# Blocks 1 to 3 of a streaming encoder layer: the mixer's input projection computed as pairs of seven half-size products

## The chip, the core and the metric

The kernel runs on one core of a Trainium2 chip. A core has TensorE (PE, matrix products into PSUM), VectorE (DVE), ScalarE (ACT), GpSimd (POOL), and SyncE (SP), which here issues the loads. Each engine works through its own queue in order; they meet only at semaphores. The metric is device time of one execution in microseconds, the median of several runs.

## What is computed

One layer over 2048 prompt frames and 32 sample frames, model width 1024, all in float32:

```
n = rmsnorm(x) * g_mix
pool_in 512 | q 512 | k 128 | v 128 | gate_p 1024 | gate_a 1024 = n @ w_in      (3328 columns)
pool = trailing means over 2/4/8/16 frames minus the frame, @ w_pool, * pool_scale
attn = chunked attention with sinks (8 heads, 2 KV heads, chunks of 64), own and previous chunk
h = x + (sigmoid(gate_p) * pool + sigmoid(gate_a) * (attn @ w_attn_up)) @ w_out
h = h + relu(rmsnorm(h) @ w_up)^2 @ w_down                                       (hidden 4096)
y = rmsnorm(h) * g_fin
```

The reference also returns the newest keys, values and pooling inputs.

## The kernel before, in words

Features lie on partitions, frames along the free axis. The prompt is cut into four blocks of 512 frames; block 0 also carries the 32 sample frames (544 columns). Each block runs a mixer (everything up to h) and then an MLP.

Every float32 operand of a product is split in a high and a low part: ScalarE copies it rounded (`split_high`, `copy`), VectorE subtracts (`split_low`, `low`), and TensorE makes three products, high x high, high x low, low x high (`three`, line 512 for the matmuls).

**The mixer** (`mixer_product`, `step`, list `MIXER`) goes through 42 units: 26 tiles of the input projection, 8 of attention up together with the pooling product, 8 of the output. A unit's weights are 128x1024 (or 128x640), loaded by SP into one of four raw places, split into one of two slots of `wm`, and multiplied by `nH`, `nL` (x times g_mix, split). A tile of the input projection takes 8 x 3 matmuls of 512 columns; its result is scaled by the inverse root `rms` when VectorE takes it out of PSUM (`scale_gate`, `xp_out`); q and k are copied and rotated with tables scaled by `rms`. Attention steps lie between the units (`between`).

**The MLP of block 0** is made of plain products of the same kind. Meanwhile GpSimd forms sums of quarters of the MLP's weights (`sum_weights`), two units to a sum of four quarters, ScalarE and VectorE split part of them, and ScalarE's queue writes them to `weight_sums` and `weight_split` in memory.

**The MLP of blocks 1 to 3** uses a Strassen-like scheme: a pair of weight tiles and both halves of frames and of input features give seven products of half size instead of eight. One such product is a token: 4 x 3 matmuls of 256 columns (lines 731 to 733). A phase has 28 tokens (`ORDER`), there are eight phases (four up, four down). Weights come through a ring of eight places `wring`; a token's raw quarter is 128x512, split by ScalarE eight tokens ahead and by VectorE seven ahead, unless it was written split. Operands are combined from quarters and split (`n7H`, `n7L`, `m7H`, `m7L`). Seven products of a pair pass through three pieces of PSUM, and products 6, 3, 7, 4 wait for what ScalarE copied or VectorE added of the products before.

During the last down phase the next block's x is prepared: squares, inverse root (`invert_part`), x times g_mix split into `nH`, `nL` (`gained_low`, line 1229), angles scaled. GpSimd multiplies y of a finished block by its inverse root (line 1686) at the start of the next mixer and does the pooling.

Of the kernel before, what the change touches and what calls it, by code (L numbers as in the profile page):

```python
# [6 lines left out]
F32 = mybir.dt.float32  # L7
F32R = mybir.dt.float32r
ALU = mybir.AluOpType
# [35 lines left out]
def mixer_plan(out_order):  # L45
    plan = [("qkv", m) for m in range(6)] + [("xp", m) for m in range(G)] + [("gp", m) for m in range(KD)]
    for m in range(KD):
        plan += [("ga", m), ("ao", m)]
    return plan + [("out", m) for m in out_order]


MIXER = mixer_plan(range(KD))
PLAN = [MIXER] + [mixer_plan(ORD)] * (NB - 1)
# [5 lines left out]
ROPE_LOAD = 16  # L59
# [4 lines left out]
Y_STORES = (2, 3, 4, 5)  # L64
POOLED = KD - G
ATT0 = 7

# [15 lines left out]
HALF = (0, 0, 1, 0)  # L83
SHIFT = (0, 4, 0, 4)
# [3 lines left out]
def presplit(ph, pr):  # L88
    return ph in SPLIT_PHASES and pr in (5, 6, 7)


def build(nc, x0, x123, weights, consts, vectors, tables, state_s, kcache_t, vcache, kold, vold,
          y0, y123, k_new, v_new, p_new, k_old_out, v_old_out, ks_new, vs_new, ps_new):
    with ExitStack() as ctx:
# [26 lines left out]
        def own(name, shape, dt=F32):  # L121
# [22 lines left out]
        rope = place("rope", [P, 2, CMAX], n_tail)  # L144
        qbuf = place("qbuf", [P, NJ * CMAX], n_tail + 8 * CMAX)
        pr = place("pr", [P, 2, 4 * P], n_tail + 24 * CMAX)
        prT = place("prT", [P, 2, 4 * P], n_tail + 24 * CMAX + 4096)
        n7H, n7L = (place(f"n7{x}", [P, 7, PAIRS, HT], at_n + i * n7_bytes, F32R) for i, x in enumerate("HL"))

        midH, midL = place("midH", [P, KD, CMAX], at_m, F32R), place("midL", [P, KD, CMAX], at_m + n_bytes, F32R)  # L150
        m_tail = at_m + 2 * n_bytes
# [5 lines left out]

        half_bytes = RING * QW * 4
        wring = place("wring", [P, RING, 2, QW], at_w, F32R)
        wm = [place(f"wm{h}", [P, 2, 2, WIDTH], at_w + h * half_bytes, F32R) for h in range(2)]  # L160
        xbs = [place(f"xb{h}", [P, 3, XWMAX], at_w + h * half_bytes) for h in range(2)]
        diffs = [place(f"diff{h}", [P, XWMAX], at_w + h * half_bytes + 12 * XWMAX) for h in range(2)]
# [15 lines left out]
        qC = qbuf[:, 0:NJ * TB].rearrange("p (c j n) -> p c j n", c=NC, j=NJ)  # L178
        qS = qbuf[:, NJ * TB:].rearrange("p (j n) -> p j n", j=NJ)
# [50 lines left out]
        set_out = [sem(f"set_out{i}") for i in range(2)]  # L230
        prod_done = sem("prod_done")
# [22 lines left out]
        plain = [("x", 0), ("h", 0)] + [("x", b) for b in later]  # L254
        s_nH = Signal("gained_high", [(*n, k) for n in plain for k in range(KD)])
        s_nL = Signal("gained_low", [(*n, k) for n in plain for k in range(KD)])
        s_tab = Signal("angles_scaled", [(b,) for b in blocks])
        s_fg = Signal("final_gained", [(b, tile_at("f", b, k)) for b in blocks[:-1] for k in range(KD)])
        s_y = Signal("y_normed", [(b, k) for b in blocks for k in range(KD)])
        s_tmp = Signal("qk_copied", [(b, i) for b in blocks for i in range(NJ + 1)])  # L260
        s_vn = Signal("v_normed", [(b,) for b in blocks])
# [5 lines left out]
        s_xb = Signal("pool_in_copied", groups)  # L267
# [15 lines left out]
        s_gz = Signal("gate_scaled", [(b, kind, m) for b in blocks for kind in ("gp", "ga") for m in range(KD)])  # L283
# [15 lines left out]
        s_SL = Signal("weight_sums_low", split_pairs)  # L299


        out_pairs = [(b, j) for b in later for j in range(PAIRS)]
        s_g = Signal("h_gained", [(b, m) for b in later for m in ORD])
        s_gT1, s_gT3, s_gT2, s_gT4 = (Signal(f"h_{n}", out_pairs) for n in ("T1", "T3", "T2", "T4"))
        s_gH2, s_gL2, s_gH5, s_gL5 = (Signal(f"h_{n}", out_pairs) for n in ("first_high", "first_low", "rest_high", "rest_low"))
# [16 lines left out]
        splits = []  # L322
        for b in blocks:
            splits += [("mix", b, i) for i in range(M_MLP)]
            if b == 0:
                splits += [("plain", 0, n) for n in range(2 * KD * NQ)]
            else:
                splits += [("tok", b, t) for t in range(TOKENS) if not presplit(t // NT7, ORDER[t % NT7][1])]
# [13 lines left out]
        for b in later:  # L342
            for t in range(TOKENS):
                if presplit(t // NT7, ORDER[t % NT7][1]):
                    landed[(t + SHIFT[b]) % RING] += 16
                    ring_count[b, t] = landed[(t + SHIFT[b]) % RING]
        set_count, landed = {}, [0, 0]
        for p in range(PHASES * PAIRS):
            landed[p % 2] += 32 if p // PAIRS in SPLIT_PHASES else 16
            set_count[p] = landed[p % 2]  # L350

        def is_split(b, t):
            return presplit(t // NT7, ORDER[t % NT7][1])

        def raw_tokens(b, lo, hi):
            return [t for t in range(lo, hi) if t < TOKENS and not is_split(b, t)]

        def ring_slot(b, t):
            return (t + SHIFT[b]) % RING
# [9 lines left out]

        def unit_row(b, i):  # L370
            return MIXER.index(PLAN[b][i])

        def mlp_row(q, down, tile):
            return M_MLP + 2 * KD * q + KD * down + tile

# [1452 lines left out]
```

## Time and profile before

| | us |
|---|---|
| median of 3 runs | 2358.72 (2357.66 to 2358.92) |
| profiled execution | 2357.24 |
| its span | 2355.5 |

| engine | busy in the span |
|---|---|
| PE | 2325.8 (99%) |
| DVE | 1642.3 (70%) |
| ACT | 1091.6 (46%) |
| POOL | 388.0 (16%) |

The span runs from the first to the last instruction. Matmuls are pipelined: the time of one row of a matmul is longer than the distance between two starts, and the distance is what counts. An engine's mean share says nothing of single stretches.

### The profile page before, as it was taken

What the parts mean: (1) busy time and instruction counts of PE and PEld (TensorE: products, weight loads), DVE (VectorE), ACT (ScalarE), POOL (GpSimd) and SP (SyncE); (2) the same over time, 40 slices, a digit from 0 to 9 for tenths busy, and PEclk for the clock granted to TensorE, in tenths of its full rate; (3) what the DMA queues carried; (4) which work ended last, traced back from release to release, by engine and by line L of the source; (5) the groups of instructions that cost most, each with busy time, mean ns of one, the idle gap of its engine ahead of it and who ended that gap; (6) DMA issues with size and microseconds to landing.
All of it is one profiled execution on the core that took longest, in us unless ns stands there. A gap on an engine that the chain in (4) does not pass through costs nothing.

```text
span 2355.5 us, 41198 instructions
## 1 busy us (share of the span) xinstructions
PE 2325.8 (99%) x16389; PEld 2159.7 (92%) x16389; DVE 1642.3 (70%) x2438; ACT 1091.6 (46%) x1922; POOL 388.0 (16%) x296
## 2 busy tenths in 40 slices
PE   8999999999999999999999999999999999999997
PEld 8999999999987889999987788999998778999996
DVE  7645766465885568778687557876788656867866
ACT  4533434233535346456554435654463534645542
POOL 0500364563634000000013200000003400000000
PEclk9999999999999999999999999999999999999998
DMA  4223465565652237767653235767674223676774
GB/s 161 78 74 101 170 225 187 202 240 179 220 192 66 87 116 246 237 202 230 226 201 117 76 103 171 229 226 246 200 264 145 77 88 114 206 228 200 237 231 169
DMA packets 149167, 410.38 MB, mean 174 GB/s; under 512 B 17521, under 2 KB 17873, under 8 KB 144881
## 3 DMA queue, kind: packets, MB, share of 16 engines
q1 hardware_dynamic: 136752, 349.71, 45.2%
q10 hardware_dynamic: 12224, 58.04, 6.6%
q8 instruction: 131, 2.15, 0.4%
q14 instruction: 60, 0.48, 0.1%
HBM read 349.65 MB, written 58.13 MB: 173 GB/s over the span
## 4 chain that ended last, share of the span: by engine, by line
PE 94%; DVE 3%; DMA 2%; ACT 0%; issue 0%; POOL 0%; SPq 0%; DVEq 0%; ACTq 0%; POOLq 0%
PE prod L512 50%; PE auxB L731 8%; PE auxB L733 8%; PE auxB L732 8%; PE prod L731 6%; PE prod L732 6%; PE prod L733 6%; DMA wring<-weight_split 1%; PE auxB L512 1%; PE auxA L614 1%; PE auxB L644 1%; PE auxB L628 1%; DVE acc L1211 0%; PE auxA L512 0%; DVE wm L1188 0%
## 5 line engine op out<-in xcount | busy, mean ns | idle before, releaser
L512 PE MATMUL prod<-nH,wm 128*128 128x272 f32 (+1 forms) x3104 | 718.7, 333 | 7.9 <-DVE nL L1229 7.9
L512 PEld LDWEIGHTS prod<-nH,wm 128*128 128x128 f32 x3104 | 497.9, 188 | 67.9 <-DVE wm L1188 8.1
L775 ACT ACTIVATE wm<-raw 128x1024 fp32r<-128x1024 f32 x232 | 235.7, 1016 | 667.2 <-PE prod L512 660.9
L512 PE MATMUL prod<-nL,wm 128*128 128x272 f32 (+1 forms) x1552 | 438.4, 331 | 0.0
L775 ACT ACTIVATE wring<-rawq 128x512 fp32r<-128x512 f32 x492 | 303.2, 628 | 273.1 <-PE auxB L733 170.1
L1188 DVE TENSOR_TENSOR wring<-rawq,wring 128x512 fp32r<-128x512 f32 x492 | 334.6, 684 | 99.9 <-PE auxB L733 78.3
L1188 DVE TENSOR_TENSOR wm<-raw,wm 128x1024 fp32r<-128x1024 f32 x232 | 305.2, 1316 | 59.5 <-ACT wm L775 58.7
L512 PE MATMUL prod<-midH,wm 128*128 128x272 f32 (+1 forms) x1664 | 335.0, 313 | 2.1 <-DVE midL L1188 1.6
L512 PEld LDWEIGHTS prod<-nL,wm 128*128 128x128 f32 x1552 | 263.4, 189 | 26.6 <-issue 0.5
L512 PEld LDWEIGHTS prod<-midH,wm 128*128 128x128 f32 x1664 | 253.2, 188 | 20.2 <-DVE midL L1188 1.8
L731 PE MATMUL auxB<-m7H,wring 128*128 128x256 f32 x768 | 218.2, 284 | 3.0 <-DMA wring<-weight_split 2.9
L731 PE MATMUL auxB<-n7H,wring 128*128 128x256 f32 x768 | 218.2, 284 | 0.0
L733 PE MATMUL auxB<-n7H,wring 128*128 128x256 f32 x768 | 217.4, 283 | 0.0
L732 PE MATMUL auxB<-n7L,wring 128*128 128x256 f32 x768 | 217.4, 283 | 0.0
L732 PE MATMUL auxB<-m7L,wring 128*128 128x256 f32 x768 | 217.4, 283 | 0.0
L733 PE MATMUL auxB<-m7H,wring 128*128 128x256 f32 x768 | 217.3, 283 | 0.0
L512 PE MATMUL prod<-midL,wm 128*128 128x272 f32 (+1 forms) x832 | 208.3, 313 | 0.0
L1686 POOL TENSOR_TENSOR hT<-hT,acc 128x512 f32<-128x512 f32 (+1 forms) x24 | 42.1, 1788 | 949.4 <-DVE acc L1216 949.4
L731 PE MATMUL prod<-m7H,wring 128*128 128x256 f32 x576 | 164.3, 285 | 0.1
L731 PE MATMUL prod<-n7H,wring 128*128 128x256 f32 x576 | 164.2, 285 | 0.0
L733 PE MATMUL prod<-n7H,wring 128*128 128x256 f32 x576 | 163.0, 283 | 0.0
L732 PE MATMUL prod<-n7L,wring 128*128 128x256 f32 x576 | 163.0, 283 | 0.0
(174 smaller groups left out, 4521.1 us busy)
## 6 DMA issues: line engine op xcount, KB each, us to landing
raw<-weights SPq DMA_DIRECT2D x200, 512.0 KB, 3.5
wring<-weight_split SPq DMA_DIRECT2D x180, 512.0 KB, 4.4
rawq<-weights SPq DMA_DIRECT2D x288, 256.0 KB, 4.3
rawq<-weight_sums SPq DMA_DIRECT2D x204, 256.0 KB, 4.2
weight_split<-wsplit ACTq DMA_DIRECT2D x20, 1536.0 KB, 5.9
weight_sums<-wsum ACTq DMA_DIRECT2D x12, 1024.0 KB, 5.7
raw<-weights SPq DMA_DIRECT2D x32, 320.0 KB, 2.8
y<-hT ACTq DMA_DIRECT2D x12, 512.0 KB, 2.8
```

Of the source, the lines that this page charges most:

```text
L512: ins = nc.tensor.matmul(out[:, s, 0:hi - lo], lhs, rhs[:, lo:hi], start=first, stop=last)
L614: ins = nc.tensor.matmul(bank[:, at:at + P], q, keys[:, :, t * CH:(t + 1) * CH], start=True, stop=True)
L628: ins = nc.tensor.transpose(auxB[:, 1, i * P:(i + 1) * P], pr[:, c % 2, i * P:(i + 1) * P], ident)
L644: ins = nc.tensor.matmul(auxB[feats, 0, 0:2 * P], v[:, c // 2, feats], prT[:, c % 2, 2 * g * P:2 * (g + 1) * P], start=True, stop=True)
L731: nc.tensor.matmul(out, wh, xh, start=kp == 0 and r in (1, 2, 5), stop=False, skip_group_check=True)
L732: nc.tensor.matmul(out, wh, xl, start=False, stop=False, skip_group_check=True)
L733: ins = nc.tensor.matmul(out, wl, xh, start=False, stop=kp == PAIRS - 1, skip_group_check=True)
L775: return nc.scalar.activation(out, in_, ACT.Copy, scale=scale)
L1188: return tt(out, x, f(high), ALU.subtract)
L1686: tt(hT[:, k, 0:n], hT[:, k, 0:n], acc[:, 0:n], ALU.mult).then_inc(s_y.sem, 1)
```

## The change

In blocks 1 to 3 the 26 tiles of the input projection become 13 pairs (`WIN`) of seven products of 256 columns. The MLP's ring now runs through the mixer too: 123 tokens, 91 of these products, 8 for pooling, 8 for attention up, 16 halves of output tiles, in an order given by keys (`mixer_tokens`). Places such as `ROTATE_AT` and `ATT_AT` say after which token the rotations and attention steps come.

GpSimd forms four sums for each of 13 pairs during block 0's mixer (`sum_mix_weights`), and ScalarE's queue writes them out unsplit; they are split in the ring like any quarter. For that block 0 orders its gates in pairs, x's place and others serve as working places, and x is loaded a second time (`x_again`) before the output products, in each block.

x is first multiplied by its inverse root on GpSimd (`norm_x`, 8 tiles; at the end of block 0 four of them stand behind each of the weight sums 28 and 29 of 0 to 31), then by the gain, and combined and split in seven operand parts in the last down phase. Products are therefore no longer scaled when they are taken out; results are put together from copies by ScalarE and additions by VectorE in place. The MLP's presplit sums go out in two transfers, high and low.

```diff
+WIN = [("qkv", 0), ("qkv", 2), ("qkv", 4), ("xp", 0), ("xp", 2)] + [("gp", m) for m in (0, 2, 4, 6)] + [
+    ("ga", m) for m in (0, 2, 4, 6)]
+OFFSET = {1: 0, 2: 1, 5: 2, 6: 3, 3: 5, 7: 6, 4: 11}
+def mixer_tokens():
+    for p in range(NPAIR):
+        for r, off in OFFSET.items():
+            keyed.append((1.4 + 0.1 * r if p == 1 and r in (1, 2) else 7 * p + off, ("win", p, r)))
...
+ATT_AT = [place_of(31 + 4 * n) for n in range(NC + 2)]
+ROTATE_AT = [place_of(key) for key in (7, 13, 15, 20, 23)]
+GAIN_AT = (13, 16, 19, 22)
...
+            def win_token(b, i, p, r):          # TensorE
+                weights_here(b, i)
+                if r == 1:
+                    if p >= 2:
+                        wait(pe, s_m3, b, p - 2)
...
+                if r == 2 and p >= 2:
+                    wait(pe, s_m01, b, p - 2)
+                if r in (5, 6, 3, 7, 4) and r != 5:
+                    wait(pe, {6: s_m1, 3: s_m5, 7: s_m0, 4: s_m2}[r], b, p)
...
+            def win_step(b, p, r):              # ScalarE
+                if r == 1:
...
+                    elif p == 2:
+                        wait(act, s_q, b, 1)
...
+                    copy(first[:, HT:TB], mix_a(p)).then_inc(s_m1.sem, 1)
...
+            def win_step(b, p, r):              # VectorE
+                if r == 3:
+                    tt(first, first, prod[p % 2][:, 1, :], ALU.add).then_inc(s_m01.sem, 1)
+                if r == 7:
+                    tt(second[:, 0:HT], second[:, 0:HT], mix_a(p), ALU.add).then_inc(s_m2.sem, 1)
+            def mixer_step(b, i):               # VectorE
...
+                weights_ahead(b, i)
...
+                if i == 4:
+                    invert("f", b - 1)
+                if i in ROTATE_AT:
+                    rotate(b, ROTATE_AT.index(i))
...
             def down_step(b, q, k):             # VectorE, last down phase
-                    if k % 2 and 7 <= k < 7 + 2 * KD:
-                        gained_low("x", b + 1, (k - 7) // 2)
+                    for j, at in enumerate(GAIN_AT):
+                        if k == at:
+                            gain_first("x", b + 1, j)
+                        if k == at + 1:
+                            gain_rest("x", b + 1, j)
+                            gain_first_low("x", b + 1, j)
+                        if k == at + 2:
+                            gain_rest_low("x", b + 1, j)
...
+            for p in range(PHASES * PAIRS):     # GpSimd, block 0's MLP
+                sum_weights(p)
+                if p >= PHASES * PAIRS - 4 and p < PHASES * PAIRS - 2:
+                    for m in ORD[0:4] if p % 2 == 0 else ORD[4:8]:
+                        norm_x(1, m)
...
+                    act.wait_ge(set_out[1], set_count[PHASES * PAIRS - 1])   # ScalarE, end of block 0
+                    for at in raw_tokens(1, 4, RING):
+                        split_high_token(*at)
```

## Rows read from the trace of the kernel before

In the view of stretches (rows 3) the columns are the stretch, its length, busy us and instructions of PE, PEld, DVE, ACT and POOL, PE's granted clock, the DMA share and GB/s. In timelines they are start, us, engine, line, instruction, count, and idle time before with its releaser.

**Rows 1.** The page, first part: busy us, share of the span, instructions
```profile
PE 2325.8 (99%) x16389; PEld 2159.7 (92%) x16389; DVE 1642.3 (70%) x2438; ACT 1091.6 (46%) x1922; POOL 388.0 (16%) x296
```
**Rows 2.** Waits of TensorE: waiting, releaser, us in total, times, longest
```profile
PE prod L512 <- DVE nL L1229: 7.9, 1, 7.9
```
**Rows 3.** Stretches: mixer 0, MLP 1, mixer 2, last down phase of block 1
```profile
24.00:213.00 189.00, 189.00 (x1511) 181.90 (x1510) 114.55 (x186) 70.01 (x164) 36.28 (x46) 1.00 0.26 83
888.37:1216.26 327.89, 325.99 (x2693) 323.64 (x2692) 255.54 (x451) 184.62 (x326) 0.00 (x0) 1.00 0.72 235
1216.26:1451.08 234.82, 234.82 (x1072) 184.80 (x1071) 153.34 (x219) 97.36 (x191) 45.08 (x38) 1.00 0.30 99
1176.00:1216.30 40.30, 38.50 (x317) 37.90 (x316) 34.07 (x60) 24.39 (x38) 0.00 (x0) 1.00 0.67 243
```
**Rows 4.** Timeline of TensorE: start, us, instruction; 24 matmuls of 512 columns, twelve of 256
```profile
888.37 0.28 PE L731 MATMUL auxB<-n7H,wring 128*128 128x256 f32 x1
...
889.81 0.28 PE L731 MATMUL prod<-n7H,wring 128*128 128x256 f32 x1
...
1216.26 0.40 PE L512 MATMUL prod<-nH,wm 128*128 128x512 f32 x1
...
1221.83 0.59 PE L512 MATMUL auxA<-acc,ones 128*128 128x512 f32 x1
```
**Rows 5.** Groups by form, whole span: busy us, mean ns, idle before, releasers
```profile
L1188 DVE TENSOR_TENSOR wring<-rawq,wring 128x512 fp32r<-128x512 f32 x492 | 334.6, 684 | 99.9 <-PE auxB L733 78.3 <-ACT wring L775 12.2 <-PE prod L733 8.9
L775 ACT ACTIVATE wring<-rawq 128x512 fp32r<-128x512 f32 x492 | 303.2, 628 | 273.1 <-PE auxB L733 170.1 <-PE prod L733 67.6 <-DMA rawq<-weights 25.7
L1188 DVE TENSOR_TENSOR wm<-raw,wm 128x1024 fp32r<-128x1024 f32 x200 | 279.0, 1395 | 59.2 <-ACT wm L775 58.7
L775 ACT ACTIVATE wm<-raw 128x1024 fp32r<-128x1024 f32 x200 | 212.0, 1060 | 594.0 <-PE prod L512 587.6 <-DMA raw<-weights 3.3 <-PE auxB L733 3.0
L1594 DVE TENSOR_TENSOR hT<-hT,auxB 128x256 f32<-128x256 f32 x192 | 79.8, 415 | 51.6 <-PE auxB L733 50.4
L775 ACT ACTIVATE zt<-auxB 128x256 f32<-128x256 f32 x96 | 36.8, 383 | 49.8 <-PE auxB L733 42.4 <-DVE m7L L1188 7.3
L1188 DVE TENSOR_TENSOR n7L<-zt,n7H 128x1280 fp32r<-128x1280 f32 x12 | 17.9, 1493 | 7.1 <-ACT n7H L775 6.7
L1308 DVE TENSOR_TENSOR hT<-prod,rms 128x512 f32<-128x512 f32 x24 | 16.6, 691 | 39.0 <-PE prod L512 39.0
L1666 POOL TENSOR_TENSOR wsum<-wsum,raw 128x512 f32<-128x512 f32 x32 | 62.8, 1962 | 2.5
```
**Rows 6.** The same view of the last down phase of block 2 (1725 to 1771)
```profile
L1229 DVE SCALAR_TENSOR_TENSOR nL<-xT,vec,nH 128x512 fp32r<-128x512 f32 x8 | 6.0, 744 | 0.0
```
**Rows 7.** Timeline of VectorE and GpSimd at the start of block 2
```profile
1223.18 1.23 DVE L1188 TENSOR_TENSOR wm<-raw,wm 128x1024 fp32r<-128x1024 f32 x1 [0.96 <-ACT wm L775]
1224.33 3.35 DVE L1216 RECIPROCAL acc<-acc 128x512 f32<-128x512 f32 x1
1229.61 1.77 DVE L1188 TENSOR_TENSOR wm<-raw,wm 128x1024 fp32r<-128x1024 f32 x1 [1.94 <-ACT wm L775]
...
1233.01 1.78 DVE L1253 TENSOR_TENSOR work<-work,rope 128x512 f32<-128x512 f32 x1
...
1244.81 0.69 DVE L1252 TENSOR_TENSOR work<-work,rope 128x512 f32<-128x512 f32 x1
...
1227.75 13.84 POOL L1686 TENSOR_TENSOR hT<-hT,acc 128x512 f32<-128x512 f32 x8 [464.71 <-DVE acc L1216]
```
**Rows 8.** Timelines of GpSimd, VectorE and TensorE at the end of block 0
```profile
636.89 1.29 POOL L1665 TENSOR_TENSOR wsum<-raw 128x512 f32<-128x512 f32 x1 [2.41 <-DMA weight_split<-wsplit]
...
642.62 2.83 DVE L1188 TENSOR_TENSOR wsplit<-wsum,wsplit 128x1536 fp32r<-128x1536 f32 x1
...
647.36 0.49 PE L512 MATMUL prod<-midH,wm 128*128 128x272 f32 x2 [0.55 <-DVE wm L1188]
```
**Rows 9.** The page, part six: issues, KB each, median us to landing
```profile
weight_split<-wsplit ACTq DMA_DIRECT2D x20, 1536.0 KB, 5.9
```

More of the change, by code:

```diff
@@ L58 @@
 RAW = 4
-ROPE_LOAD = 16
 K_HALF = TB // 2 + CH
@@ L319, in wait @@
             eng.wait_ge(signal.sem, signal.count[item])
[L322 to L328, printed above, removed]
+        splits = [("mix", 0, i) for i in range(M_MLP)] + [("plain", 0, n) for n in range(2 * KD * NQ)]
+        for b in later:
+            splits += [("tok", b, i) for i in range(TT) if not presplit(i)]
         split_no = {item: n + 1 for n, item in enumerate(splits)}
@@ new lines, in whole, with pool_token @@
+            def whole(out, b, i, k, high, low, first, last):
+                wh, wl = (wring[:, ring_slot(b, i), h, k * P:(k + 1) * P] for h in range(2))
+                nc.tensor.matmul(out, wh, high, start=first, stop=False)
+                nc.tensor.matmul(out, wh, low, start=False, stop=False)
+                return nc.tensor.matmul(out, wl, high, start=False, stop=last)
+            def pool_token(b, i, m):
+                weights_here(b, i)
+                if m == 0:
+                    wait(pe, s_aL, b, NC - 1)
+                if m >= 2:
+                    wait(pe, s_pool, b, m - 2)
+                g = m // 2
+                wait(pe, s_pL, b, g)
+                whole(auxB[:, m % 2, :], b, i, 0, midH[:, POOLED + g, 0:TB], midL[:, POOLED + g, 0:TB],
+                      True, True).then_inc(prod_done, 1)
@@ new lines, in step_0 @@
+                if kind == "out":
+                    wait(act, s_h, 0, m)
+                    gained_high("h", 0, m)
+                    square("h", 0, m, hT)
+                if i == 6:
+                    copy_v(0)
+                attention(0, i - ATT0)
+                if i - 1 in SUM_UNITS:
+                    mix_sums_out(SUM_UNITS.index(i - 1))
+                if i in (8, 12, 16, 20):
+                    pooled_high(0, (8, 12, 16, 20).index(i))
+                if i == 22:
+                    store_carry(0)
@@ new lines, in step_0 @@
+                attention(0, i - ATT0)
+                if i + 2 < M_MLP:
+                    split_low(i + 2)
+                else:
+                    split_low_plain(i + 2 - M_MLP)
+                if kind == "out":
+                    gained_low("h", 0, m)
+                    add_square("h", 0, m)
+                if kind == "ao":
+                    merged_low(0, m)
+                if i == 0:
+                    invert("x", 0)
+                if i == 1:
+                    scale_angles()
@@ new lines, in _ @@
+            for b in later:
+                wait(pool, s_r, "f", b - 1)
+                for k in range(KD):
+                    n = cols(b - 1)
+                    wait(pool, s_fg, b - 1, k)
+                    tt(hT[:, k, 0:n], hT[:, k, 0:n], acc[:, 0:n], ALU.mult).then_inc(s_y.sem, 1)
+                for g in range(G):
+                    pooling(b, g)
+                    pooled_low(b, g)
+                if b + 1 < NB:
+                    for m in ORD:
+                        norm_x(b + 1, m)
```

1139 lines of the change are left out of this document (690 added, 449 removed).

## The prediction

> **What bounds the kernel now.** I read the page first: TensorE is busy 99% of the span, VectorE 70%, ScalarE 46% [rows 1]. The list of waits shows that TensorE waits for almost nothing: the longest group is one wait of 7.9 us at the start [rows 2]. So the order of matmuls sets the time, as long as the others keep up. The table of stretches says how near they are to not keeping up [rows 3]: in the mixer of a later block (234.8 us) VectorE works 153 us; in an MLP of 328 us it works 256; in the last down phase before a new block (40.3 us) it works 34.1. A change that takes matmuls away and gives VectorE work is decided in the stretches where VectorE has no room.
>
> **TensorE.** Blocks 1 to 3 compute 26 input tiles each with 24 matmuls of 512 columns: 624 a block. The starts of 24 of them lie 1221.83 - 1216.26 = 5.57 us apart, 0.232 us each [rows 4]. Afterwards 13 pairs x 7 products x 12 matmuls = 1092 of 256 columns; twelve of these start 889.81 - 888.37 = 1.44 us apart, 0.120 each [rows 4]. 144.8 us become 131.0: 13.7 us less a block, 41 us in all (not 12.5% of 144.8, since two halves cost 0.240 where one whole costs 0.232). Attention up, pooling and output products keep their number and width, and block 0 keeps all of its own. TensorE's granted clock is 1.00 in all these stretches, its upper level, and I assume no loss there.
>
> **VectorE, splits of weights.** The operand in two parts (high, low) costs a ScalarE copy and a VectorE subtraction per unit. A mixer had 34 wide ones at 1.40 us [rows 5] and 8 of 640 elements, in proportion 0.9: 55 us. Now 91 + 16 + 8 quarters at 0.684 and 8 small ones at some 0.25: 81 us, 26 more a block. On ScalarE 41 us (34 at 1.06, 8 in proportion) become 74 (115 at 0.628, and 8 small), and copies of products out of PSUM add four at 0.38 a pair, 20 us a block [rows 5]. ScalarE goes from 97 of 235 us to some 145 of 221: room left, and no cost put on it by itself. Gates and inputs scaled by the norm (21 at 0.69) go, 13 pairs of additions (0.684 + 0.415) come: even. In total VectorE has about 153 + 26 = 179 us of work in 221. That fits on average; three places don't.
>
> **Place 1, the last down phase of blocks 1 and 2.** Of the 34.1 us in 40.3 [rows 3] go eight gained tiles (0.744 each here, 6.0 [rows 6]) and a wide split, 7.4 together. Added: for each of four pairs the sums (four of 128x256, 0.42 each), a subtraction of 512 (0.68) and one of 1280 (1.49) [rows 5], 3.85 a pair, 15.4; and the splits of the next block's first seven tokens, 4.8. That makes 46.9 us of work in 40.3: 6.6 too many, before any waiting in it. Beside it GpSimd now multiplies eight x tiles by the norm, at 1.73 each (eight of the same kind take 13.84 us [rows 7]), 14 us. Its cost for VectorE shows where GpSimd normalises y: a multiplication in the rotation takes 1.78 where it takes 0.69 later, a split 1.77 where it took 1.23 [rows 7]. Over those 13.8 us eight such operations lose 5.3, 0.65 each, by their rows in that stretch. The same over 14 us here is 5.4 more: 12.0. The ring of eight weights lets TensorE run ahead only where no accumulation waits for VectorE, and in a down phase each product r 6, 3, 7, 4 waits for the addition of the one before in its bank. So nearly all of it becomes waiting. TensorE waited 1.8 us there already, part of which is in it. I take 11 us for each of the two, bounds 5 and 15: 22.
>
> The Trainium skill (SBUF — State Buffer, "SBUF: two separate sides") says that VectorE with two SBUF inputs and a reading GpSimd instruction lock each other out for a whole instruction. By that rule all of GpSimd's 14 us would be lost to VectorE; the trace agrees in kind (0.69 becomes 1.78), not in full (5.3 of 13.8). With the whole of it the sum would be that of the last rival below, 2416; with the measured share it stays 2375.
>
> **Place 2, the first pairs of each mixer.** From token 4 on VectorE has: the reciprocal of the final norm in one piece (3.35 us [rows 7]), splits of tokens 12 to 19 (8 x 0.61 back to back), two additions each for pairs 0 and 1 (1.9), and the rotations of q tiles 0 and 1 (2.7 each without GpSimd). That is 15.5 us, to which GpSimd's eight y tiles add some 14 x 0.65 = 9. ScalarE's copy of pair 2's first product waits for the second rotation, since pair 2 takes the place of pair 0, and the fourth product of pair 2 (token 16) waits for that copy. From the end of token 4 to token 16 TensorE has 11 tokens, 15.8 us. Root, waits and two splits ahead take 3 us more of it. 15.5 + 9 + 3 - 15.8 = 11.7 at full contention, 2.7 with none; some of the operations fall beside gaps in GpSimd's work. A further 1 to 2 us goes at attention's first steps, where one step keeps ScalarE 5 us and two tokens hang on its copies. I take 8 a block, bounds 0 and 12: 24 for three blocks. ScalarE waits behind that copy, and the splits of tokens 21 and 22 behind it.
>
> **Place 3, the end of block 0.** Before, GpSimd's last sum starts at 636.9 and takes 7 us [rows 8]. Now two groups of four x tiles (7.5 us each) stand between the last sums, the first behind the reciprocal. ScalarE's step for each pair waits for the sum and stands ahead of the next unit's split; the last pair's sum ends some 10 us later (644 to 653). VectorE is full here already: a subtraction of 1536 takes 2.83 with GpSimd beside it (1.75 without), and TensorE has a wait of 0.55 us there [rows 8]. I walk the queue: the splits of the last two units 1 and 3 us late; the low parts of the last sums written at about 669; six us for their transfer (5.9 [rows 9]), and only then may tokens 4 and on be split, since they lie on those sums' place. Token 4 starts near 677 instead of 665. Cost 10 us, bounds 3 and 15.
>
> **What hides.** The 13 sums of mixer weights (four operations each, the longest 1.96 on the mean [rows 5], 6.8 us together, 88 in all) lie in block 0's mixer, where GpSimd is busy 36 of 189 us and VectorE 115 [rows 3]; each pair has its weights summed one to three units before ScalarE sends them. Contention adds perhaps 25 us to VectorE's 115, and it keeps room; 1 us taken, bounds 0 and 6. If that cover were gone, loads would wait for sums, at 7 us a pair. The x tiles loaded again (2 MB a block, needed at the output products, issued some 30 tokens earlier) and 178 GB/s of weights in the mixer are under the 235 GB/s that the MLP moves now [rows 3]: nothing. On SP's queue each of these stands ahead of weight loads, but eight raw places are full by then.
>
> **Sum.** -41 + 22 + 24 + 10 + 1 = +16 us against the profiled execution's 2357.24: 2373; its time is 1.5 us under the median of the runs, so 2375. By the bounds alone: -41 + 10 + 0 + 3 + 0 = -28 (2331), and -41 + 30 + 36 + 15 + 6 = +46 (2405).
>
> **Rivals.**
> - The matmuls' saving comes through nearly whole, because VectorE catches up in its gaps: it idles 6 us in each last down phase, and GpSimd's contention falls on operations that nobody awaits. Then places 1 to 3 cost 5, 1 and 4 each: -41 + 10 + 3 + 4 + 1 = -23, 2336. For it: MLP phases run at 78% of VectorE without a wait. Against it: 46.9 in 40.3 can't be caught up. Chance 0.2.
> - Contention halves and the rotation just meets its token: -41 + 16 + 9 + 7 + 1 = -8, 2351. Chance 0.1. Between this and the forecast lies no change: 0.05.
> - Worse than forecast: the loads. A raw place comes free only by VectorE's split of the token eight before; when VectorE is late by over 4 tokens, a load (some 4 us from issue to landing) is late as well, and each backlog costs that again. It decides if VectorE's backlog passes about 5 us in places 1 and 2, five places in all; at 4 us each 20 us more: 2395. Against it: loads are issued in order long ahead when TensorE waits too. Chance 0.08.
> - GpSimd shuts VectorE out for all of its time: place 1 loses 6.6 + 14.2 - 1 = 20 twice, place 2 14 three times: -41 + 40 + 42 + 15 + 1 = +57, 2416. Against it: multiplications of 0.99 beside GpSimd in the same stretch. Chance 0.02.
>
> **Chances.** Forecast (2362 to 2390) 0.55. A difference of under 0.2%, 5 us, is what can't be told from none. Faster by more: 0.2 + 0.1 = 0.3; within: 0.05; slower: 0.65. The range is 2332 to 2395: below it lies a part of the first rival, above it the last and half of the loads.
>
> **What would show it.** Right: matmuls on the ring of 256 columns, 1092 more a block, 0.120 apart; TensorE's waits of 50 to 70 us in the list, for VectorE's additions in the last down phases of blocks 1 and 2 and for ScalarE's copy some 16 tokens into each mixer; VectorE over 90% busy there; rotations of 5 us under GpSimd's y; a gap of 5 to 12 us at the first tokens of block 1. Wrong: a mixer of 221 us with no wait in it, a last down phase of 40 us, or waits for loads. If mixers take 221 to 223 us and down phases 41, the first rival is true and the kernel is faster.

## The result, and the profile after

The changed kernel takes 2418.15 us (median of four runs, 2416.3 to 2422.2) against 2358.19 (four runs, 2357.6 to 2358.9) for the kernel before on the same chip: ratio 1.0254, 95% interval 1.0241 to 1.0267. It is 60 us slower. The forecast was 2375, range 2332 to 2395: the direction was right, the size was outside the range.

The page's first part, to be read against [rows 1]:

```profile
PE 2310.3 (96%) x17793; PEld 2226.7 (92%) x17793; DVE 1795.5 (74%) x2741; ACT 1227.6 (51%) x2330; POOL 507.8 (21%) x372
```

TensorE's share fell from 99 to 96%. The list of its waits has the reasons (waiting, releaser, us in total, times, longest); in the kernel before only the wait at the start [rows 2] was over 3 us:

```profile
PE prod L793 <- ACT zm L971: 27.4, 4, 8.4
PE auxB L924 <- DVE hT L1947: 20.0, 7, 4.0
PE prod L621 <- DVE wm L1486: 16.6, 5, 4.4
PE prod L621 <- DVE nL L1532: 8.0, 1, 8.0
PE auxA L621 <- DVE acc L1514: 5.8, 2, 3.0
PE prod L793 <- ACT hT L971: 4.6, 6, 1.0
PE auxB L924 <- DMA wring<-weight_split: 3.8, 6, 1.2
```

The first row is place 2, the second place 1, the third mostly place 3; waits for loads (the last row) stayed small, so the rival of late loads did not come. In place 2 ScalarE's copy, for which TensorE waits, itself waits for VectorE to finish a rotation (ScalarE's list of waits):

```profile
ACT zm L971 <- DVE qbuf L1573: 33.7, 3, 11.6
```

Stretches of the changed kernel: block 0's mixer, last down phase of block 1, mixer of block 2 whole and in halves (compare [rows 3]):

```profile
24.00:213.00 189.00, 182.49 (x1439) 174.56 (x1438) 133.35 (x180) 68.81 (x160) 110.16 (x95) 0.99 0.42 147
1222.62:1262.92 40.30, 30.35 (x217) 29.35 (x215) 37.48 (x59) 27.65 (x42) 11.93 (x8) 0.87 0.57 191
1262.92:1497.11 234.19, 224.27 (x1540) 202.89 (x1539) 185.10 (x302) 134.48 (x316) 47.64 (x38) 0.98 0.49 152
1262.92:1380.00 117.08, 107.16 (x859) 100.61 (x858) 101.16 (x163) 71.35 (x197) 47.64 (x38) 0.96 0.52 159
1380.00:1497.11 117.11, 117.11 (x683) 102.27 (x682) 83.95 (x140) 63.13 (x120) 0.00 (x0) 1.00 0.46 145
```

The same halves of that mixer before the change:

```profile
1216.26:1333.30 117.04, 117.04 (x565) 89.69 (x564) 80.26 (x120) 50.35 (x128) 45.08 (x38) 1.00 0.29 97
1333.30:1451.08 117.78, 117.78 (x508) 95.11 (x508) 73.08 (x99) 47.02 (x63) 0.00 (x0) 1.00 0.31 100
```

VectorE's 185 us in 234 look like room. They are 101 of 117 in the first half, where GpSimd works too, and 84 of 117 in the second, where TensorE never waits. The mean over the mixer hid how little room its first half has.

The second thing to see is TensorE's clock. Its timeline at the longest wait of block 2 (start, us, instruction, idle before and releaser):

```profile
1287.35 0.28 PE L795 MATMUL prod<-n7H,wring 128*128 128x256 f32 x1
1295.60 0.55 PE L793 MATMUL prod<-n7H,wring 128*128 128x256 f32 x1 [7.97 <-ACT zm L971]
1295.95 0.41 PE L794 MATMUL prod<-n7L,wring 128*128 128x256 f32 x1
1296.16 0.42 PE L795 MATMUL prod<-n7H,wring 128*128 128x256 f32 x1
```

Behind the wait the matmuls start 0.21 us apart instead of 0.12. In stretches of 5 us the granted clock is 0.66, 0.50 and 0.82 there: the lower of its two levels, 1.2 instead of 2.4 GHz, for about 6 us behind a wait of 8. A stretch at clock c loses 1 - c of its length, but at most half of the time that TensorE was busy in it. Summed over all stretches of 5 us that is 25.1 us, against 0.6 in the kernel before.

**Where 60.7 us of span come from.** Two ways of counting agree. By kind: TensorE's waits add up to 92.5 us against 16.4 (+76), the lower clock takes 24.5 more, the matmuls save 41: +59. By place, from the first matmul of each stage:

| | before | after | cost beyond the matmuls' saving | of it lower clock | forecast |
|---|---|---|---|---|---|
| block 0 | 653.5 | 681.2 | 27.8 | 8.4 | 10 + 1 |
| mixers of blocks 1, 2, 3 | 234.9, 234.8, 234.8 | 240.1, 234.2, 233.2 | 44.0 | 7.4 | 24 |
| MLPs of blocks 1, 2 | 327.9, 326.5 | 341.6, 341.7 | 28.8 | 8.3 | 22 |
| MLP of block 3 and end | | | 1.2 | 1.0 | 0 |

### The profile page after: what moved, and what is told of

It reads as the page before. It is cut to its first block, busy times and chain, and to the rows that moved or that the text cites. A ratio compares the mean times of both kernels' runs of the same rounds, so it can differ in the third digit from the quotient of the medians.

```text
span 2416.2 us, 45625 instructions
## 1 busy us (share of the span) xinstructions
PE 2310.3 (96%) x17793; PEld 2226.7 (92%) x17793; DVE 1795.5 (74%) x2741; ACT 1227.6 (51%) x2330; POOL 507.8 (21%) x372
## 4 chain that ended last, share of the span: by engine, by line
PE 76%; DVE 13%; issue 4%; ACT 3%; DMA 2%; POOL 1%; SPq 0%; DVEq 0%; ACTq 0%; POOLq 0%
PE prod L621 19%; PE auxB L924 7%; PE auxB L925 7%; PE auxB L926 7%; PE prod L924 5%; PE prod L925 5%; PE prod L926 5%; DVE wring L1486 3%; PE prod L793 3%; PE prod L794 3%; PE prod L795 3%; PE prod L801 2%; PE prod L802 2%; PE prod L800 2%; ACT pr L1021 1%
## 5 line engine op out<-in xcount | busy, mean ns | idle before, releaser
L971 ACT ACTIVATE wring<-rawq 128x512 fp32r<-128x512 f32 (+1 forms) x861 | 525.8, 620 | 405.8 <-PE auxB L926 170.1
L1486 DVE TENSOR_TENSOR wring<-rawq,wring 128x512 fp32r<-128x512 f32 (+1 forms) x861 | 613.4, 722 | 128.1 <-PE auxB L926 77.9
L793 PE MATMUL prod<-n7H,wring 128*128 128x256 f32 x1092 | 317.6, 291 | 35.9 <-ACT zm L971 27.4
L621 PE MATMUL prod<-nH,wm 128*128 128x272 f32 x1856 | 315.7, 291 | 12.4 <-DVE nL L1532 8.0
L795 PE MATMUL prod<-n7H,wring 128*128 128x256 f32 x1092 | 311.5, 285 | 0.0
L621 PEld LDWEIGHTS prod<-nH,wm 128*128 128x128 f32 x1856 | 264.8, 190 | 14.2 <-DVE wm L1486 12.8
L793 PEld LDWEIGHTS prod<-n7H,wring 128*128 128x128 f32 x1092 | 212.1, 194 | 43.8 <-issue 32.2
L621 PE MATMUL prod<-midH,wm 128*128 128x272 f32 x1280 | 219.1, 293 | 12.5 <-DVE wm L1486 12.2
L794 PEld LDWEIGHTS prod<-n7L,wring 128*128 128x128 f32 x1092 | 212.4, 195 | 1.4 <-issue 0.5
L795 PEld LDWEIGHTS prod<-n7H,wring 128*128 128x128 f32 x1092 | 212.3, 194 | 0.0
L621 PE MATMUL prod<-nL,wm 128*128 128x272 f32 x928 | 193.2, 290 | 0.0
L1486 DVE TENSOR_TENSOR wm<-raw,wm 128x1024 fp32r<-128x1024 f32 (+1 forms) x106 | 149.2, 1407 | 43.1 <-ACT wm L971 42.6
```

The source lines that it names most:

```text
L621: ins = nc.tensor.matmul(out[:, s, 0:hi - lo], lhs, rhs[:, lo:hi], start=first, stop=last)
L793: nc.tensor.matmul(out, wh, xh, start=kp == 0 and r in (1, 2, 5), stop=False, skip_group_check=True)
L794: nc.tensor.matmul(out, wh, xl, start=False, stop=False, skip_group_check=True)
L795: ins = nc.tensor.matmul(out, wl, xh, start=False, stop=kp == PAIRS - 1, skip_group_check=True)
L971: return nc.scalar.activation(out, in_, ACT.Copy, scale=scale)
L1486: return tt(out, x, f(high), ALU.subtract)
```

## Experiments

Sixteen runs, each timed beside the kernel before. Where an operation is put on 16 columns it keeps its place and its waits but takes almost no time; such a version gives other results and only serves to measure. The table gives each one's excess over that kernel's median on its own chip; the 95% interval of each ratio reaches about 0.0015 to each side (3.5 us).

| kernel | us | over before | against the changed kernel's +60.0 |
|---|---|---|---|
| GpSimd's y on 16 columns | 2394.07 | +36.1 | -24 |
| GpSimd's x on 16 columns | 2399.97 | +42.0 | -18 |
| both, and 10 of 13 sums of mixer weights | 2369.53 | +11.6 | -48 |
| filler matmuls in a wait | 2414.99 | +57.1 | -3 |
| final norm later | 2423.73 | +64.6 | +5 |
| x behind the sums in block 0 | 2411.04 | +51.9 | -8 |
| final norm later, place 1 eased | 2420.22 | +61.1 | +1 |
| these three together | 2411.87 | +52.7 | -7 |
| y in pieces of 128 columns | 2404.78 | +45.9 | -14 |
| y on VectorE | 2414.18 | +55.3 | -5 |
| y on VectorE, other orders | 2405.05 | +46.1 | -14 |
| x and gained sums on 16 columns | 2395.41 | +36.5 | -23 |
| y and x in pieces, x behind the sums | 2391.79 | +32.1 | -28 |
| VectorE relieved | 2359.07 | -0.6 | -61 |
| y on VectorE, stores later | 2414.48 | +54.3 | -6 |
| the same, x in pieces and behind the sums | 2402.50 | +42.3 | -18 |

**1. GpSimd's multiplications made narrow.**

```diff
-    tt(hT[:, k, 0:n], hT[:, k, 0:n], acc[:, 0:n], ALU.mult).then_inc(s_y.sem, 1)
+    tt(hT[:, k, 0:16], hT[:, k, 0:16], acc[:, 0:16], ALU.mult).then_inc(s_y.sem, 1)
```

> GpSimd's multiplication of each y tile by the final norm is done on 16 columns instead of all (this leaves y of blocks 0 to 2 unnormalised). Theory A: beside GpSimd's 14 us VectorE's operations last 1.0 to 1.8 instead of 0.7, and that is most of the wait of 8 us before the fourth product of pair 2 (token 16). Then three waits of 8 fall to under 3 and TensorE's clock does not fall behind them: 2418 - 3 x 5.5 - 3 x 3 = 2393, range 2386 to 2400. Rival B: the wait is VectorE's own queue (reciprocal in one piece, splits, two rotations in order), GpSimd adds little: waits stay over 6 us and the time is 2410 to 2418.

Measured 2394.07: theory A, within 1 us. The wait before token 16 falls from 7.97 to 1.78 us in block 2, mixers 2 and 3 from 234.2 and 233.2 to 226.3 and 225.6.

```diff
-    tt(xT[:, m, 0:TB], xT[:, m, 0:TB], rms[:, 0:TB], ALU.mult).then_inc(s_xr.sem, 1)
+    tt(xT[:, m, 0:16], xT[:, m, 0:16], rms[:, 0:16], ALU.mult).then_inc(s_xr.sem, 1)
```

> GpSimd's multiplication of each x tile by the norm is done on 16 columns (this leaves the mixer's input of blocks 1 to 3 unnormalised). Theory A: in the last down phases of blocks 1 and 2 half of the waits (9.7 and 10.4 us) was contention and goes, 5 us each, with 2 us of the lower clock each; at the end of block 0 eight multiplications of 1.5 to 1.9 no longer stand between the last sums and the sums no longer hold up ScalarE's splits: 10 to 14 us. Together 2418 - 14 - 12 = 2392, range 2384 to 2400. Rival B: VectorE has 6.6 us too much work in these phases with no help from GpSimd, and block 0's last sums wait for loads anyway: waits of 8 and more stay, 2405 to 2415.

Measured 2399.97, at the very end of theory A's range. Block 0 ends 9.4 us earlier, but the MLPs get only 2.7 and 3.9 us shorter: in the last down phase contention was the smaller part.

```diff
-    sums(mix_set(p)[0], ..., s_MS)
+    sums(mix_set(p)[0], ..., s_MS, QW if p in (0, 1, 10) else 16)
```

> Both of the above, and 10 of the 13 sums of mixer weights in block 0 on 16 columns (leaves out y's norm, x's norm and those sums). Theory A: all of GpSimd's new load is gone; what remains is VectorE's own surplus in the two last down phases (3 to 6 us each), the end of block 0 (5 to 10), and place 2 (0 to 3 each): 2418 - 25 - 26 - 6 = 2361, range 2345 to 2370. Rival B (VectorE's own work is the bound, GpSimd only shifts it): 2385 or more.

Measured 2369.53, theory A at the upper end of its range. 24 + 18 leaves 6 to 7 us for the sums in block 0's mixer, and the trace has them: block 1 starts 7.3 us earlier than with x alone narrow. With nearly all of GpSimd's new load gone (three sums remain) the kernel still isn't faster than before.

**2. The clock.** 56 matmuls whose result nobody reads stand in the wait of each mixer.

```diff
+    if (p, r) == (2, 6):
+        for _ in range(56):
+            nc.tensor.matmul(auxB[:, 1, 0:HT], wring[:, ring_slot(b, i), 0, 0:P], n7H[:, QUAD[r], 0, :], ...)
```

> Adds 56 matmuls of 256 columns (6.7 us at 0.12) into an unused bank before the fourth product of pair 2 in each of three mixers, in the wait of 8 us. No waiting is taken away. Theory C: TensorE's clock falls to its lower level in that wait and stays there some 5 us after it, at 3 us of loss per block; with the filler it stays up: 2418 - 3 x 3 = 2409, range 2406 to 2412. Rival D: the slow matmuls behind the wait (0.21 to 0.24 apart) come from something else, or the wait itself grows by the filler: 2418 or more.

Stretches of 5 us at the place, first the changed kernel, then this one:

```profile
1285.00:1290.00 5.00, 2.62 (x22) 2.42 (x21) 4.93 (x4) 0.00 (x0) 4.60 (x3) 1.00 0.24 77
1290.00:1295.00 5.00, 0.00 (x0) 0.00 (x0) 4.90 (x10) 0.00 (x0) 0.00 (x0) 0.66 0.61 191
1295.00:1300.00 5.00, 4.41 (x20) 4.44 (x21) 4.51 (x8) 3.12 (x7) 0.00 (x0) 0.50 0.42 143
1300.00:1305.00 5.00, 5.00 (x37) 5.00 (x37) 3.44 (x7) 2.17 (x4) 0.00 (x0) 0.82 0.75 221
```

```profile
1290.00:1295.00 5.00, 4.93 (x41) 4.73 (x40) 4.52 (x10) 2.05 (x5) 0.00 (x0) 1.00 0.49 137
1295.00:1300.00 5.00, 5.00 (x44) 5.00 (x43) 4.90 (x9) 3.12 (x7) 0.00 (x0) 1.00 0.76 224
1300.00:1305.00 5.00, 5.00 (x44) 5.00 (x43) 4.90 (x10) 2.52 (x6) 0.00 (x0) 1.00 0.89 303
```

The clock stays at 1.00 here and the slow matmuls are gone, so rival D's other cause for them falls. But the mixers shorten by 2.6, 1.8 and 0.9 us, 5.3 of the 7.4 that the clock costs there, and the median, 2414.99, lies between the two ranges: 3 us less, which its interval hardly tells from nothing. The saving was smaller for two reasons that the trace shows in part. TensorE meets the next wait with more of it left (0.56 becomes 1.00 us at attention); that VectorE catches up while TensorE is slow is my reading of it. And in the two MLPs, which were not touched, the lower clock costs 11.7 us in this execution instead of 8.3. The Trainium skill (TensorE: Matmul & The Clock Gate, "HAM oscillation — how this bites in real kernels") describes the same for waits for transfers: after them the matmuls go on at the lower clock. The rows above agree, here behind a wait for ScalarE, and the prediction had left it out.

**3. How VectorE and GpSimd take turns.** VectorE and GpSimd at place 2 of the changed kernel (timeline, block 2):

```profile
1276.49 0.67 DVE L1723 TENSOR_TENSOR zm<-zm,prod 128x512 f32<-128x512 f32 x1
1278.54 3.14 DVE L1486 TENSOR_TENSOR wring<-rawq,wring 128x512 fp32r<-128x512 f32 x2
1283.31 1.79 DVE L1564 TENSOR_TENSOR zm<-zm,rope 128x512 f32<-128x512 f32 x1
1285.13 1.66 DVE L1573 TENSOR_TENSOR qbuf<-zm 128x512 f32<-128x512 f32 x1
1286.82 3.33 DVE L1486 TENSOR_TENSOR wring<-rawq,wring 128x512 fp32r<-128x512 f32 x2
1293.56 0.68 DVE L1564 TENSOR_TENSOR zm<-zm,rope 128x512 f32<-128x512 f32 x1
```

```profile
1276.11 13.49 POOL L2114 TENSOR_TENSOR hT<-hT,acc 128x512 f32<-128x512 f32 x8 [38.90 <-DVE acc L1519]
```

Most operations with both inputs in SBUF last 1.6 to 1.8 us, which is one of GpSimd's (13.49 / 8 = 1.69) and no more: one for one. The addition with an input in PSUM (first row) lasts its 0.67 in the midst of it. So such an operation loses up to 1.69 - 0.68 = 1.0 us to one GpSimd instruction (which lasts 1.28 us where VectorE is idle, at 638 us of the same trace). Eight operations of VectorE have two SBUF inputs in these 13.5 us; some start beside a gap and lose less, and together they lose 6.8 us. If the two engines take turns by instruction, shorter instructions must help:

```diff
-    tt(hT[:, k, 0:n], hT[:, k, 0:n], acc[:, 0:n], ALU.mult).then_inc(s_y.sem, 1)
+    for at in range(0, n, P):
+        ins = tt(hT[:, k, at:min(at + P, n)], hT[:, k, at:min(at + P, n)], acc[:, at:min(at + P, n)], ALU.mult)
+    ins.then_inc(s_y.sem, 1)
```

> Nothing is left out. GpSimd's multiplication of each y tile is issued as four of 128 columns in place of one of 512. Theory A (the two engines take turns, instruction by instruction, and an operation of VectorE waits for the whole one of GpSimd beside it): VectorE's operations beside y last 0.69 + 0.4 instead of 0.69 + 1.0, y takes 25 to 35 us instead of 14, and the wait before token 16 shrinks from 8 to 3 to 5 us: 2418 - 3 x 4 - 3 = 2403, range 2396 to 2410. Rival B (both engines slow each other by a share of bandwidth): the same y work costs VectorE the same in total, the wait stays 7 to 8 us, 2416 to 2422.

Measured 2404.78: theory A. The same two engines:

```profile
1275.21 1.02 DVE L1563 TENSOR_TENSOR zm<-zm,rope 128x512 f32<-128x512 f32 x1
1276.15 0.95 DVE L1564 TENSOR_TENSOR zm<-zm,rope 128x512 f32<-128x512 f32 x1
1277.13 0.83 DVE L1573 TENSOR_TENSOR qbuf<-zm 128x512 f32<-128x512 f32 x1
1278.00 1.71 DVE L1486 TENSOR_TENSOR wring<-rawq,wring 128x512 fp32r<-128x512 f32 x2
```

```profile
1270.96 23.84 POOL L2116 TENSOR_TENSOR hT<-hT,acc 128x128 f32<-128x128 f32 x32 [38.91 <-DVE acc L1519]
```

Each of VectorE's operations waits 0.15 to 0.35 us and not 1.0; GpSimd needs 24 us instead of 13.5, which nobody awaits. From the first addition (zm, prod) to the end of the second rotation VectorE needs 18.5 us in the changed kernel, 14.0 here and 11.8 with y on 16 columns; TensorE's wait is 8.0, 3.9 and 1.8. So y costs VectorE 6.7 us here whole and 2.2 in pieces. The Trainium skill (SBUF — State Buffer, "SBUF: two separate sides") calls it a lock held for the whole instruction; these rows agree in kind. The prediction read the rule as all of GpSimd's time lost; since the engines take turns, it is half of it, 6.8 of 13.5 us.

**4. Final norm later.**

```diff
-Y_AT = [place_of(key) for key in (13, 17, 21, 25)]
+Y_AT = [place_of(key) for key in (20, 23, 26, 29)]
-    if i == 4:
+    if SUM_F < i <= SUM_F + NT:        # SUM_F = 10
-        invert("f", b - 1)
+        invert_part("f", b - 1, i - SUM_F - 1)
```

> Nothing is left out. The final norm of the block before (sum of squares, root, reciprocal in four parts, GpSimd's y) begins at token 11 of the mixer instead of token 4, y is stored and the pooled tiles are taken some tokens later. Theory A: the wait of 8 us before token 16 is the meeting of the reciprocal and of GpSimd's y with the first two rotations; once they are apart it goes as it went with y on 16 columns: 2418 - 24 = 2394, range 2388 to 2400. Rival B: y now lies beside the other three rotations, gate tiles wait for y's store, and the wait only moves: 2405 to 2418.

Measured 2423.73: a miss, and worse than rival B. The wait before token 16 did go (1.55 us are left), but waits of 0.6, 2.1 and 4.4 us come behind it, the last at attention's first step, before which ScalarE waits 3.2 us for a weight load and 2.0 for VectorE. With one of 1.2 later that is about 10 us in the mixer of block 2, as before. The lost time moved; the full first half of the mixer explains it, though no run here takes that apart.

**5. The end of block 0.**

```diff
-    if p >= PHASES * PAIRS - 4 and p < PHASES * PAIRS - 2:
-        for m in ORD[0:4] if p % 2 == 0 else ORD[4:8]:
+    if p >= PHASES * PAIRS - 3 and p < PHASES * PAIRS - 1:
+        for m in ORD[0:4] if p % 2 else ORD[4:8]:
```

> Nothing is left out. At the end of block 0 GpSimd multiplies the two groups of four x tiles behind the last sums but two and but one, instead of one sum earlier each. Theory A: GpSimd now idles 7.5 us for the reciprocal with a sum of weights queued behind it, and ScalarE waits 9 us for that sum: with the sum ahead of the wait, block 0's end gets 8 to 12 us shorter, 2406 to 2410. Rival B: VectorE's own work with 1.4 to 1.5 us for each 256-column sum beside GpSimd sets this stretch whatever the order: 0 to 4 us, 2414 to 2418.

Measured 2411.04, 8 us less on its own comparison, at theory A's end. GpSimd and ScalarE in the changed kernel, then GpSimd here:

```profile
625.63 7.41 POOL L2084 TENSOR_TENSOR xT<-xT,rms 128x512 f32<-128x512 f32 x4 [7.48 <-DVE rms L1519]
633.00 1.28 POOL L2019 TENSOR_TENSOR set_s<-raw 128x512 f32<-128x512 f32 x1
...
638.28 1.48 ACT L971 ACTIVATE set_h<-set_s 128x1536 fp32r<-128x1536 f32 x1 [9.02 <-POOL set_s L2022]
```

```profile
621.20 1.29 POOL L2019 TENSOR_TENSOR set_s<-raw 128x512 f32<-128x512 f32 x1 [4.05 <-DMA weight_split<-set_l]
...
627.94 6.04 POOL L2084 TENSOR_TENSOR xT<-xT,rms 128x512 f32<-128x512 f32 x4
```

GpSimd stood idle 7.5 us for the reciprocal with the next sum behind it, and ScalarE waited 9 us for that sum. The sum now starts at 621 instead of 633 and block 1 at 672.5 instead of 681.2, as early as with x on 16 columns (671.8). That kernel kept the idle time of 7.5 us and only had the multiplications short (its sum starts at 626), so either remedy alone takes away what x cost in block 0.

**6. The last down phases.**

```diff
-GAIN_AT = (13, 16, 19, 22)
+GAIN_AT = (10, 14, 18, 22)            # and the reciprocal at k 2 to 5 instead of 6 to 9
+    if b > 1 and i in (0, 2, 4, 6):    # in the next mixer, VectorE one token later
+        final_square(b - 1, 4 + i // 2)
```

> The later final norm, and in the last down phases of blocks 1 and 2 four of eight final squares (ScalarE) and their additions (VectorE, 0.7 each) go into the first 8 tokens of the next mixer, the reciprocal begins 4 tokens earlier and the gained tiles 3, 2, 1 and 0 tokens earlier. Theory A: VectorE has 6.6 us too much in that phase, 3 of them leave it and its idle time at the start is used: waits of 10 us fall to about 5, with 1 to 2 us of the lower clock, in two blocks: 13 below the kernel with the later final norm alone, 2381, range 2375 to 2388. Rival B: what leaves the phase is missing in the next mixer's first tokens: 2390 to 2396.

> All three together. Theory A: the places are separate and add up: 2418 - 24 - 13 - 10 = 2371, range 2362 to 2378, still over the kernel before, because VectorE's own work in the last down phases and the sums beside it in block 0 remain. Rival B: above 2380.

Measured 2420.22, outside both ranges, and 2411.87, rival B. Against the later final norm alone the MLPs shorten by 2.8 and 1.1 us only; the waits of the phase change places (a first one of 5.5 us instead of 4.0). The order at block 0's end adds its 8 us. Both lie on the final norm's later place, which was itself a loss.

```diff
+    w = 16 if kind == "x" and b > 1 else HT
-    tt(z(j, 2, 3), z(j, 1, 2), z(j, 0, 1), ALU.subtract)
+    tt(z(j, 2, 3)[:, :, 0:w], z(j, 1, 2)[:, :, 0:w], z(j, 0, 1)[:, :, 0:w], ALU.subtract)
```

> GpSimd's multiplication of x by the norm and VectorE's four sums per pair of gained tiles (blocks 2 and 3) on 16 columns (leaves out the norm of x and most of those sums). Theory A: in the last down phases VectorE has more work than time; 16 sums of 0.42 us become 0.1, 5 us less in each of two phases, and an MLP of 338 us (with x's norm alone on 16 columns) falls to 332 or 333: 2400 - 11 = 2389, range 2385 to 2393. Rival B: the waits there come from the order of additions and not from the amount of work: 2396 to 2400.

Measured 2395.41, between the two ranges: about 5 us less than with x alone narrow, where A wanted 11. The MLPs last 334.6 and 337.1 us instead of 338.9 and 337.8. Then the low parts were made narrow as well:

```diff
+    w = 16 if kind == "x" and b > 1 else HT
-    low(n7L[:, 2:7, j, :], z(j, 3, 8), n7H[:, 2:7, j, :])
+    low(n7L[:, 2:7, j, 0:w], z(j, 3, 8)[:, :, 0:w], n7H[:, 2:7, j, 0:w])
```

> As the kernel with GpSimd's y, x and sums on 16 columns, and besides all of VectorE's sums and low parts of the gained x tiles of blocks 2 and 3 on 16 columns (leaves out both norms, most sums and most of the low parts of the mixer's input). Theory A: it is the amount of VectorE's work: with 3.3 us less a pair, 13 us a phase, the waits of 8 us go and the MLPs of blocks 1 and 2 last 328 to 330 us as before the change: 2369.5 - 18 = 2352, range 2347 to 2356, below the kernel before. Rival B: it is the order of the additions and of ScalarE's steps between them: MLPs of 334 us or more, 2361 or more.

Measured 2359.07, between A and B, and no different from the kernel before (1.0000, 0.9990 to 1.0009). The last 40.3 us of block 1's last down phase, with x alone narrow and here:

```profile
1210.30:1250.60 40.30, 31.54 (x227) 30.52 (x227) 35.15 (x64) 27.79 (x43) 1.48 (x8) 0.88 0.67 226
```

```profile
1187.60:1227.90 40.30, 35.68 (x289) 34.87 (x289) 31.10 (x76) 30.51 (x48) 1.48 (x8) 1.00 0.75 254
```

The MLPs last 331.2 and 335.6 us, against 338.4 and 337.3 with GpSimd's load alone gone: 7.2 us shorter in block 1, 1.7 in block 2. TensorE's waits shrink in both (9.1 to 4.6 us, 8.9 to 5.5); what differs is the clock. A wait of 2.9 us for an addition is left in both, and behind it the granted clock stays at 1.00 in block 1 and falls in block 2:

```profile
1225.00:1230.00 5.00, 5.00 (x42) 5.00 (x43) 4.64 (x10) 4.32 (x8) 0.00 (x0) 1.00 0.47 122
1785.00:1790.00 5.00, 5.00 (x26) 5.00 (x26) 2.71 (x6) 2.20 (x5) 0.00 (x0) 0.53 0.54 160
```

With a second fall behind a wait of 2.2 us for a load, the lower clock costs 4.8 us in the MLP of block 2 and nothing in that of block 1, which is the difference between them (4.4 us). So VectorE's amount of work makes about 4 us of waiting in each of places 1; whether the clock falls behind a wait of 2 to 3 us is not settled by its length, and no run shows what decides it.

**7. Y by VectorE.** The expectations count GpSimd's eight multiplications as 8.2 us taken from VectorE. Doing them itself costs it 5.5 us, which should be cheaper.

```diff
-    wait(pool, s_r, "f", b - 1) ...    # GpSimd's loop over the y tiles
+    if i in Y_TILE:                    # keys 17, 20, 23, 26, 30, 33, 37, 40, on VectorE
+        tt(hT[:, k, 0:n], hT[:, k, 0:n], acc[:, 0:n], ALU.mult).then_inc(s_y.sem, 1)
```

> Nothing is left out. VectorE multiplies the y tiles itself, 8 operations of 0.69 us spread over keys 17 to 40 of the mixer's order, the final norm's reciprocal in four parts behind the second rotation; GpSimd does none of it. Theory A: beside GpSimd each of its 8 multiplications takes 1.0 us from VectorE, 8.2 us in all, so that doing them costs VectorE less (5.5) than being helped; and spread out they meet no deadline: mixers of 226 to 230 us as with y on 16 columns, 2418 - 20 = 2398, range 2392 to 2404. Rival B: VectorE has no room in tokens 16 to 40 for 5.5 us more, attention's first steps wait as with the later final norm: 2408 to 2424.

> Nothing is left out. Y on VectorE as in the one before, the x tiles behind the last sums of block 0, and reciprocal and gained tiles begun earlier in the last down phases. Theory A: 2398 - 7 - 3 = 2388, range 2380 to 2394, above the kernel before all the same. Rival B: 2398 or more, since VectorE's work comes to the same sum in any order.

Measured 2414.18 and 2405.05: rival B both times. In the first one's trace ScalarE waits 4.3 and 6.2 us in a mixer for y tiles that it is to send, so the test was not clean; the next moves the stores three to four tokens back.

> Nothing is left out. As the kernel with y on VectorE, and each store of two y tiles three to four tokens later. Theory A: ScalarE's waits of 4.3 and 6.2 us for y tiles, behind which its copies of products and splits of weights wait, go; VectorE has room for 5.5 us of y once GpSimd takes 8 us less from it: 2414 - 12 = 2402, range 2396 to 2406. Rival B: VectorE has no room at tokens 16 to 45 in any case, attention's first steps wait: 2409 to 2416.

> Nothing is left out. Y on VectorE with the later stores, GpSimd's multiplications of x in pieces of 128 columns, and x one sum later at the end of block 0. Theory A: 2402 - 13 = 2389, range 2384 to 2393, about the kernel with both in pieces on GpSimd (2392). Rival B: 2395 to 2404.

Measured 2414.48 and 2402.50: B again. ScalarE's waits for y are gone, and it now waits for VectorE in attention's first step, TensorE behind it (timelines of ScalarE and TensorE, block 2):

```profile
1318.12 0.37 ACT L1023 ACTIVATE pr<-auxA,columns 128x128 f32<-128x128 f32 x1 [5.28 <-DVE columns L1590]
```

```profile
1320.14 0.55 PE L795 MATMUL prod<-n7H,wring 128*128 128x256 f32 x1 [4.92 <-ACT xb L973]
```

With 5.5 us less of VectorE's work, as with y on 16 columns, the same mixer takes 226.3 us; with it 232.8. Those 5.5 us come back as 6.5 (the reciprocal stands at another place too). Theory A's premise was too large besides: GpSimd's y takes 6.7 us from VectorE (section 3), not 8.2, so doing it saves VectorE 1.2 us a mixer.

**8. The mended version.** Y and x in pieces of 128 columns on GpSimd, x one sum later in block 0.

> Nothing is left out. GpSimd's multiplications of y and of x by the norm both in pieces of 128 columns, and at the end of block 0 the x tiles one sum later. Theory A (turns, instruction by instruction): y's pieces give 13 us as measured, the order 7, x's pieces 2 to 5 in places 1 and 3: 2418 - 13 - 7 - 3 = 2395, range 2388 to 2400. Rival B: x in pieces takes GpSimd twice as long, gained tiles wait for it, and the gain is lost again: 2400 to 2412.

Measured 2391.79, ratio 1.0135 (1.0120 to 1.0150): the best complete version of the change, 28 us better than the change as it was made, and 32 us slower than the kernel before. No run points to a version that beats the kernel before.

## Why the prediction was right in its sign and wrong in its size

The forecast cost was 57 us against a saving of 41; the cost was 102.

- **TensorE** (-41): right. With GpSimd's load gone and VectorE relieved the mixers of blocks 2 and 3 last 225.6 and 225.9 us, 4.5 over the 221.1 that the count gives, and 4 of these are waits that the trace lists.
- **"TensorE's granted clock is 1.00 in all these stretches, and I assume no loss there"**: the step that failed most. The waits that I forecast were themselves what lets the clock fall: 24.5 us, over half of the 45 us missed. The rows of before hardly could show it, since TensorE waited almost nowhere there, but the term was put at nothing without a reason for the waits that the change itself brings.
- **Place 2** (24): the wait before token 16 is 8.4, 8.0 and 8.0 us, 24.4 in all; with GpSimd's y out it is 1.8, where 2.7 was worked out. The mechanism and the size of this wait were right. The term was too small all the same (44.0, without the clock 36.6): the 8 us a block were to hold attention's steps too, and this one wait used them up. Attention's steps take 1.5 us a mixer, as forecast, and in mixer 1 the first tokens wait 6 us for block 0's backlog, which the prediction had not counted.
- **Place 1** (22): 28.8, of which 8.3 is the clock; 20.5 us of waiting. The size of the waits was right, their split was not: with x on 16 columns a phase gets 3 to 4 us shorter, clock and all, where contention alone was put at 5.4; taking VectorE's own surplus away gave back some 4 us of waiting in each phase, where 6.6 was worked out.
- **Place 3** (10, bounds 3 and 15): 17.7, of it 6.7 of lower clock. Three waits add up to 12.2 us (0.6 before). I had seen that ScalarE's step waits for the sum, but not that GpSimd itself waits 7.5 us for the reciprocal with that sum behind it. With the order mended block 0 ends 8.7 us earlier.
- **What hides** (1, bounds 0 and 6): 10.1, outside its bounds: the same matmuls of block 0 run that much later before place 3 begins, of it 1.7 by the clock. "Keeps room" was read off 115 of 189 us; the first rotation at 33 to 40 us had none (its operations last 1.8 us beside GpSimd's sums, with a wait of 3.3 us behind it). Two figures of the working were off without touching a term: ScalarE's sum comes to 150 us and not 145, and the mixer moves 152 GB/s, not 178.
- **Contention per operation**, 0.65 us: 0.85 on the mean in place 2 and up to 1.0, for short operations too (at place 1 sums of 256 columns last 1.2 to 1.5 instead of 0.42). The last rival (2416) gave the measured time with 40 us for places 1 and 42 for places 2; taking GpSimd's y away gave back 24 and its x about 6 in the two phases, so the number agrees by chance.

## What to carry to other kernels

A wait put on TensorE costs more than its length: count the time behind it at the lower clock too, 2 to 3 us behind each wait of 8 us here, and up to 3 behind one of 2.9. Read the room of an engine in the stretch where the new work falls, not as a mean over the stage. If GpSimd and VectorE must work at once on operands in SBUF, cut GpSimd's instructions short; here that cost nothing that is awaited and gave 14 us. Work given to GpSimd is not free for VectorE: the eight multiplications took 6.7 us from it, and would have cost it 5.5.

## What the runs showed of the hardware

- VectorE's operations with two SBUF inputs and GpSimd's alternate one for one: 0.68 becomes up to 1.66 to 1.79 beside instructions of 512 columns, 0.83 to 1.02 beside 128; an addition out of PSUM keeps its 0.67.
- The clock falls to its lower level during a wait of 8 us and comes back 4 to 6 us after it; at a wait of 4.0 us it fell as well (0.69 and 0.62 in the stretches from 1235 to 1245). Behind a wait of 2.9 us it fell once (0.53) and stayed at 1.00 once. Filling one wait with matmuls kept it at 1.00 and gave back 5.3 us of the three mixers' lengths.
